# The RWKV-7 recurrence of a hybrid encoder layer, rewritten in slots: four phases of units, sums on opposite array halves, whole 64x64 inverses

## What is computed

```python
def wkv7_scan(r, w, k, v, kk, a, reverse):
    def step(state, inp):
        r_t, w_t, k_t, v_t, kk_t, a_t = inp
        sa = jnp.einsum('bhvk,bhk->bhv', state, -kk_t)
        state = (state * w_t[:, :, None, :]
                 + sa[..., None] * (kk_t * a_t)[:, :, None, :]
                 + v_t[..., None] * k_t[:, :, None, :])
        return state, jnp.einsum('bhvk,bhk->bhv', state, r_t)
    ...
    _, y = lax.scan(step, state0, xs, reverse=reverse)
```

## Time and profile before

| | us |
|---|---|
| median of 3 runs (1201.49 to 1203.64) | 1202.27 |
| span of the profiled execution, first to last instruction | 1183.8 |
| its TensorE busy | 1136.2 (96%) |
| the `scan` stage in it, first to last matmul | 516.0 to 623.7 |
| busy in 516.00 to 623.80: TensorE, VectorE, ScalarE, GpSimd | 105.57, 78.20, 50.56, 33.78 |

### The profile page before, as it was taken

One profiled execution on the slowest core, in us unless ns is written; L12 is line 12 of the kernel. 1 busy time (PEld: TensorE's weight loads), 2 busy tenths in 40 slices (PEclk: granted clock), 3 DMA queues, 4 the chain that ended last, 5 costly groups with the idle time before them and its releaser, 6 DMA issues. The chain is left out here.

```text
span 1183.8 us, 23882 instructions
## 1 busy us (share of the span) xinstructions
PE 1136.2 (96%) x9610; PEld 630.5 (53%) x9610; DVE 559.3 (47%) x1361; ACT 309.9 (26%) x793; POOL 254.2 (21%) x330
## 2 busy tenths in 40 slices
PE   6999999999999889889999999999899999999997
PEld 5534444444444457679895455664444444455553
DVE  4349526799969465556783444563111111111111
ACT  5054123522230377744451212300000000000000
POOL 0200410030000133633300001242345511112211
PEclk9989999999999999999999999999999999999999
DMA  9320343151220373436634841359999999777333
GB/s 342 97 51 26 104 140 87 36 178 36 89 54 36 90 188 103 132 102 179 162 90 178 286 180 72 134 210 414 406 349 336 381 337 343 293 285 293 136 135 114
DMA packets 109704, 213.19 MB, mean 180 GB/s; under 512 B 36516, under 2 KB 72836, under 8 KB 105752
## 3 DMA queue, kind: packets, MB, share of 16 engines
q1 hardware_dynamic: 81480, 127.19, 30.8%
q0 software_dynamic: 20192, 52.99, 13.7%
q10 hardware_dynamic: 7920, 31.46, 7.7%
HBM read 182.43 MB, written 35.58 MB: 184 GB/s over the span
## 5 line engine op out<-in xcount | busy, mean ns | idle before, releaser
L526 PE MATMUL pj_ps<-hT,pj_w 128*128 128x512 f32 x576 | 253.8, 597 | 0.0
L526 PEld LDWEIGHTS pj_ps<-hT,pj_w 128*128 128x128 f32 x576 | 108.2, 191 | 136.0 <-issue 135.4
L1464 PE MATMUL ps_out<-w_out,mixT 128*128 128x512 f32 x256 | 112.3, 594 | 2.1 <-PEq L2693 1.8
L2309 PE MATMUL ex_py<-wd,ex_hT 128*128 128x512 f32 x256 | 113.1, 592 | 0.0
L2458 ACT ACTIVATE ex_sg<-ex_pg 128x512 f32<-128x512 f32 x16 | 9.6, 597 | 272.8 <-PE ex_pg L2363 272.8
L738 DVE RECIPROCAL mixT<-mixT 128x1024 f32<-128x1024 f32 (+1 forms) x11 | 68.9, 6262 | 24.2 <-ACT mixT L658 19.2
L1464 PEld LDWEIGHTS ps_out<-w_out,mixT 128*128 128x128 f32 x256 | 47.8, 190 | 59.5 <-issue 59.4
L2377 PE MATMUL ex_pu<-proj 128*128 128x512 f32 x176 | 78.2, 592 | 0.0
L2363 PE MATMUL ex_pg<-proj 128*128 128x512 f32 x176 | 77.6, 594 | 0.0
L2572 DVE TENSOR_TENSOR ex_hid<-ex_pu,ex_sg 128x512 f32<-128x512 f32 x16 | 11.1, 691 | 136.1 <-PE ex_pu L2377 136.1
L2309 PEld LDWEIGHTS ex_py<-wd,ex_hT 128*128 128x128 f32 x256 | 47.1, 190 | 52.8 <-issue 52.8
(11 more groups left out here) (374 smaller groups left out, 1963.1 us busy)
## 6 DMA issues: line engine op xcount, KB each, us to landing
wd<-in_moe_w_down ACTq DMA_DIRECT2D x15, 2048.0 KB, 10.2
proj<-in_moe_w_gate SPq DMA_DIRECT2D x11, 2048.0 KB, 10.6
proj<-in_moe_w_up SPq DMA_DIRECT2D x11, 2048.0 KB, 12.2
mixT<-in_moe_w_gate SPq DMA_DIRECT2D x5, 2048.0 KB, 10.8
mixT<-in_moe_w_up SPq DMA_DIRECT2D x5, 2048.0 KB, 9.9
pj_w<-in_w_in SPq DMA_DIRECT2D x18, 512.0 KB, 4.0
proj<-in_x SPq DMA_DIRECT2D x16, 512.0 KB, 10.5
products<-pj_unit POOLq DMA_DIRECT2D x4, 2048.0 KB, 9.3
```

The source lines that it names most:

```text
L526: mm = pe.matmul(ps[:, t % 2, half, :], w_tile(t)[:, n, :], s.hT[:, n, half * 512:(half + 1) * 512], start=(n == 0), stop=(n == KD - 1))
L1464: mm = pe.matmul(s.ps_out[:, t % 2, half * 512:(half + 1) * 512], s.mixT[:, k, t * P:(t + 1) * P], s.w_out[:, k, half * 512:(half + 1) * 5 ...
L2309: mm = pe.matmul(py[:, half, :], hT[:, j, :], wd[e % 2][:, j, half * 512:(half + 1) * 512], start=(j == 0), stop=(j == KF - 1))
```

## The change

It replaces `scan` and what feeds it.

- **Slots.** TensorE now goes through 64 slots, one for each unit-step, the units in turn. Slot g makes the products of unit-step g+4, the right side of g, the solution of g-1 and state and output of g-2. So a unit-step's own phases lie in slots g-4, g, g+1 and g+2, with other units' work between them.
- **Halves.** Right side, solution and output are across pairs (`across_ps`). Products and the state's sums are straight (`straight_ps`). The output leaves with its heads exchanged, which `rwkv_out` undoes in its own matmuls.
- **Whole inverses.** In slots g-3 and g-2 two more pairs of 32 columns (`half_corner`, `corner`) fill in the off-diagonal 32x32 block of the inverse. The solution is then one pair in place of three, and `LOW`'s addition on VectorE is gone.
- **Products.** The second copy of the factors with exchanged halves is gone (GpSimd's 64 loads of it too). Products are two straight pairs of 128 columns; two transposes of 64 columns are made with the constant `fold`. VectorE masks 256 columns, ScalarE copies the other 128.
- **Loads.** Factors come with two loads a step (128x2x256 in place of 128x2x192), four steps deep. The inverses of four steps come with 12 loads, in two layouts that the projection stage stores (8 stores in place of 4).
- **Moved work.** The scaling of the state before the update and two of the normalising steps go from ScalarE and VectorE to GpSimd. GpSimd also clears the inverses' tiles at the stage's start.

The core of the diff:

```diff
-             l_mask_f=384, l_mask_b=384, below=32, iota=64, limits=14, token=8, keys=VCOLS, odd=1)
+             l_mask_f=256, l_mask_b=256, below=32, iota=64, limits=14, token=8, keys=VCOLS, odd=1)
...
-                for d, src in enumerate((ti[p], am[p])):
-                    sp.dma_start(s.t_dram[p, d * 64:(d + 1) * 64], src[d * 64:(d + 1) * 64, :, :].rearrange("p i j -> p (i j)")).then_inc(t_stored, 16)
+                for d, (turned, plain) in enumerate(((ti[p], am[p]), (am[p], ti[p]))):
+                    sp.dma_start(s.t_dram[d, :, :, p].rearrange("h g u b m -> (h g) (u b) m"), turned[d * 64:(d + 1) * 64, :, :].rearrange("p i j -> p (i j)")).then_inc(t_stored, 16)
+                    sp.dma_start(s.plain_dram[d, :, :, p].rearrange("h g u m -> (h g) u m"), plain[d * 64 + d:(d + 1) * 64:2, :, :].rearrange("p i j -> p (i j)")).then_inc(t_stored, 16)
...
-                dve.tensor_copy(am[p][64:128, :, :], ti[p][64:128, :, :].rearrange("p i j -> p j i")).then_inc(finished, 1)
+                dve.tensor_copy(am[p], ti[p].rearrange("p i j -> p j i")).then_inc(finished, 1)
...
+GROUP = 4
+INVERSE_LOADS, PLAIN_LOADS = 8, 4
+GROUP_IN = 16 * (INVERSE_LOADS + PLAIN_LOADS)
+def load_factors(sp, s, i):
     row = 4 * CHUNK
     for d in range(2):
+        src = bass.AP(s.p_dram.tensor, (2 * d * NCH + step_chunk(i, d)) * P * row, [[row, P], [NCH * P * row, 2], [1, row]])
+        sp.dma_start(s.units[i % 4][:, 2 * d:2 * d + 2, :, :].rearrange("p n f t -> p n (f t)"), src).then_inc(s.unit_in[i % 4], 16)
+def group_place(i, d):
+    return i % GROUP if d == 0 else GROUP - 1 - i % GROUP
+def first_chunk(g, d):
+    return GROUP * g if d == 0 else NCH - GROUP * (g + 1)
+def load_inverses(sp, s, g, n):
+    d, (h, half) = n // 4, HALVES[n % 4]
+    src = s.t_dram[d, h, first_chunk(g, d) // GROUP].rearrange("p u b (i j) -> i (p u) b j", j=SIDE)[:, :, half, :]
+    q = 2 * (1 - h) + half
+    dst = s.inverses[g][q * SIDE:(q + 1) * SIDE, 2 * d:2 * d + 2, :, half * SIDE:(half + 1) * SIDE]
+    sp.dma_start(dst.rearrange("p n u j -> p (n u) j"), src).then_inc(s.inverse_in[g], 16)
+def load_plain(sp, s, g, n):
+    d, h = n // 2, n % 2
+    src = s.plain_dram[d, h, first_chunk(g, d) // GROUP].rearrange("p u (i j) -> i (p u) j", j=SIDE)
+    q = 2 * h + d
+    sp.dma_start(s.plain[g][q * SIDE:(q + 1) * SIDE, 2 * d:2 * d + 2, :, :].rearrange("p n u j -> p (n u) j"), src).then_inc(s.inverse_in[g], 16)
...
+            def straight(out, left, right, start, stop):
                 for p0, p1 in HEADS:
+                    mm = pe.matmul(out[p0:p1], left[p0:p1], right[p0:p1], start=start, stop=stop)
+                return mm
+            def across(out, left, right, start, stop):
                 for h, (p0, p1) in enumerate(HEADS):
                     q0, q1 = HEADS[1 - h]
+                    mm = pe.matmul(out[q0:q1], left[p0:p1], right[p0:p1], start=start, stop=stop)
+                return mm
+            def first_part(x):
+                n, i, d, p, ch = place(x)
+                if n == 0:
+                    pe.wait_ge(s.unit_in[i % 4], 32 * (i // 4 + 1))
+                if x >= NU:
+                    pe.wait_ge(copied, x - NU + 1)
+                    pe.wait_ge(s_out, x - NU + 1)
+                    pe.wait_ge(t_out, x - NU + 1)
+                f = s.units[i % 4]
+                straight(straight_ps[:, n, LT * HD:(M5 + 1) * HD], f[:, n, F_K, :], f[:, n, F_A:F_K, :].rearrange("p f t -> p (f t)"), True, True)
+            def right_side(g):
+                n, i, d, p, ch = place(g)
+                pe.wait_ge(masked, g + 1)
+                pe.wait_ge(s_out, g + 1)
+                if g >= NU:
+                    pe.wait_ge(y_out, g - NU + 1)
+                across(across_ps[:, n, W:W + HD], lm[:, i % 2, n, LT, :], vt[:, p, ch, :], True, False)
+                across(across_ps[:, n, W:W + HD], s.units[i % 4][:, n, F_A, :], st[:, n, :], False, True).then_inc(w_sum, 1)
+            def transposes(x):
+                n, i, d, p, ch = place(x)
+                f = s.units[i % 4]
+                straight(straight_ps[:, n, KT * HD:(KT + 1) * HD], f[:, n, F_K, :], s.fold, True, True)
+                straight(straight_ps[:, n, BT * HD:(BT + 1) * HD], f[:, n, F_B, :], s.fold, True, True)
+            def solution(m):
+                n, i, d, p, ch = place(m)
+                pe.wait_ge(w_out, m + 1)
+                pe.wait_ge(t_out, m + 1)
+                mm = across(u_sums(n), s.inverses[i // GROUP][:, n, group_place(i, d), :], wt[:, n, :], True, True)
+                if m + NU >= TOTAL:
                     mm.then_inc(u_sum, 1)
+            def second_part(x):
+                n, i, d, p, ch = place(x)
+                f = s.units[i % 4]
+                straight(straight_ps[:, n, CT * HD:(M1 + 1) * HD], f[:, n, F_B, :], f[:, n, F_A:F_K, :].rearrange("p f t -> p (f t)"), True, True).then_inc(prods, 1)
+            def old_output(l):
+                n, i, d, p, ch = place(l)
+                pe.wait_ge(u_out, l + NU + 1)
+                across(across_ps[:, n, Y:Y + HD], s.units[i % 4][:, n, F_R, :], st[:, n, :], True, False)
+            def half_corner(x):
+                n, i, d, p, ch = place(x)
+                if x % (NU * GROUP) == 0:
+                    pe.wait_ge(s.inverse_in[i // GROUP], GROUP_IN)
+                pe.wait_ge(masked, x + 1)
+                across(z_sums(n), lm[:, i % 2, n, CT, :], s.plain[i // GROUP][:, n, group_place(i, d), :], True, True).then_inc(u_sum, 1)
+            def corner(x):
+                n, i, d, p, ch = place(x)
+                pe.wait_ge(copied, x + 1)
+                pe.wait_ge(u_out, x + 1)
+                mm = straight(straight_ps[:, n, OFF:OFF + SIDE], z_of(n), s.inverses[i // GROUP][:, n, group_place(i, d), later(d)], True, True)
+                if x < NU:
                     mm.then_inc(y_sum, 1)
+            def outputs(l):
+                n, i, d, p, ch = place(l)
+                v, u = vt[:, p, ch, :], u_of(n)
+                straight(straight_ps[:, n, STATE:STATE + HD], lm[:, i % 2, n, KT, :], v, True, False)
+                across(across_ps[:, n, Y:Y + HD], lm[:, i % 2, n, M5, :], v, False, False)
+                straight(straight_ps[:, n, STATE:STATE + HD], lm[:, i % 2, n, BT, :], u, False, True)
+                across(across_ps[:, n, Y:Y + HD], lm[:, i % 2, n, M1, :], u, False, True).then_inc(y_sum, 1)
+            pe.wait_ge(started, 2)
+            for g in range(-AHEAD, TOTAL + 2):
+                if g + AHEAD < TOTAL:
+                    first_part(g + AHEAD)
+                if 0 <= g < TOTAL:
+                    right_side(g)
+                if g + AHEAD < TOTAL:
+                    transposes(g + AHEAD)
+                if 0 <= g - 1 < TOTAL:
+                    solution(g - 1)
+                if g + AHEAD < TOTAL:
+                    second_part(g + AHEAD)
+                if 0 <= g - 2:
+                    old_output(g - 2)
+                if 0 <= g + 3 < TOTAL:
+                    half_corner(g + 3)
+                if 0 <= g + 2 < TOTAL:
+                    corner(g + 2)
+                if 0 <= g - 2:
+                    outputs(g - 2)
...
+            def mask(x):
+                n, i, d, p, ch = place(x)
+                dve.wait_ge(prods, x + 1)
+                if x >= 2 * NU:
+                    dve.wait_ge(y_sum, x - 2 * NU + NU + 1)
+                dve.tensor_tensor(lm[:, i % 2, n, CT:BT, :].rearrange("p f c -> p (f c)"), straight_ps[:, n, MADE:MADE + BT * HD], s.l_mask[d], ALU.mult).then_inc(masked, 1)
...
+            for g in range(1 - AHEAD, TOTAL + 3):
+                if g + 3 < TOTAL:
+                    mask(g + 3)
+                if 0 <= g - 3:
+                    update(g - 3)
+                i = g // NU
+                if i < NCH:
+                    if g % NU == 2 and FINAL <= i - 1:
+                        sums(i - 1)
+                    if g % NU == 2 and FINAL <= i - 3:
+                        invert(i - 3)
+                    if g % NU == 0 and FINAL <= i - 2:
+                        spread(i - 2)
...
+            def place_corner(x):
+                n, i, d, p, ch = place(x)
+                act.wait_ge(y_sum, x + 1)
+                act.wait_ge(s_out, x + 1)
+                act.activation(s.inverses[i // GROUP][:, n, group_place(i, d), later(d)], straight_ps[:, n, OFF:OFF + SIDE], ACT.Copy).then_inc(t_out, 1)
+            def negate(g):
+                m = g - 1
+                n = m % NU
+                ahead = m + NU < TOTAL
+                act.wait_ge(u_sum, m + NU + 1)
+                if m >= 0 and ahead:
+                    dst, src = uz[:, n, 0:HD + SIDE] if n < 2 else uz[:, n, SIDE:2 * HD], across_ps[:, n, U:U + HD + SIDE]
+                elif ahead:
+                    dst, src = z_of(n)[:, 0:SIDE] if n < 2 else z_of(n)[:, SIDE:HD], z_sums(n)
+                else:
+                    dst, src = u_of(n), u_sums(n)
```

(25 more changed lines are left out.)

315 lines of the change are left out of this document (118 added, 197 removed).

## The result

The changed kernel takes 1206.4 us (20 runs, 1201.88 to 1210.57), the kernel before 1201.45 (20 runs, 1193.91 to 1205.42). The ratio is 1.0048, with an interval of 1.0032 to 1.0063: slower by half a per cent, where 1170 us and 0.89 for faster had been forecast.

What follows compares the result with a forecast made beforehand. It took one half of TensorE's array to bound the recurrence. Start 0.6, lead-in 3.0, 64 slots of 1.07, statistics 2.0 and end 1.1 make 75.2 us against 107.7, so 1170 us; range 1161 to 1176, or 1162 to 1186 with waits.

Steps and rivals of the forecast that it cites:

- TensorE's new sum: Recurrence slot: straight half 0.97 us, across half 0.77, overlapping, so the slot is the longer; 1.07 us taken with waits.
- the chains of waits: Dependences between a slot's engines: the tightest needs 0.65 us of a 0.97 us slot, so every chain fits.
- What bounds the kernel now: Recurrence before: one array half bounds it; a unit-step's pairs sum to 1.49 us, measured 1.68, the rest waits.
- That rival: Recurrence: straight and across halves take turns, slot 1.74 us, stage 119 us, time 1214 us; chance 0.08.
- Matmuls of 32 columns: Short pairs in a slot: no trace showed one; priced between 0.066 and 0.117 us each, slot 0.97 to 1.02.
- Other engines: VectorE and ScalarE in a slot: some 0.75 us with overlap and 0.95 before overlap, neither exceeding 0.97.
- Statistics, start and loads: Recurrence: statistics 2 us, GpSimd's copies at the start 0.6 us, factor loads hidden with 0.7 us to spare.
- late-factors rival: Recurrence loads: factors land late, six slots last 8.1 us, stage 94 us, time 1189 us; chance 0.05.
- The gain is given back: Behind the recurrence: a later stage does not start earlier, so the time stays the same; chance 0.03.
- The 18.5 us around it stay: Outside the profiled span: 18.5 us between span and median are unchanged, so median 1202.27 becomes 1169.8 us.
- The sum: Whole recurrence: terms add to 75.2 us against 107.7, so 32.5 us saved.

Runs made afterwards that it cites:

- lean_padded: merged_lean with one extra 32-column across matmul a slot, 256 TensorE instructions more in all; ratio to the kernel before 0.9911, stage 102.8 us.
- after_again: The changed kernel, unchanged, run and profiled a second time; 1204.99 us, ratio to the kernel before 1.0049, stage 118.0 us.
- before_again: The kernel before, unchanged, profiled a second time; 1199.72 us, stage 113.6 us.
- before_third: The kernel before, unchanged, profiled a third time; 1204.51 us, stage 113.8 us.
- merged_lean: merged without those TensorE waits that an earlier wait already covers, same matmuls; 1180.47 us, ratio to the kernel before 0.9809, stage 95.7 us.
- fewer_across: The changed kernel without the output's product of masked factors with values, one across pair a slot; only the stage is read, 111.5 us.
- merged: The changed kernel with the two transposes folded into the products, two pairs a slot fewer; 1193.32 us, ratio to the kernel before 0.9933.
- after_lean: The changed kernel with only TensorE's redundant waits dropped; ratio to the kernel before 0.9983, stage 110.9 us.
- wide: The changed kernel with 192 in place of 128 columns in each slot's first products, same instruction number; 1203.16 us, ratio to the kernel before 1.0041.
- quiet: The changed kernel with the twelve `w_out` loads moved from the stage to behind it; 1215.2 us, stage 117.0 us.
- burst: The changed kernel with 512 matmuls of 32 columns added ahead of the first slot; stage 151.5 us.

## Why the prediction was wrong

**The failed step is TensorE's new sum**, as the prediction put it: "the slot is the longer of the two: 0.97", and 64 times 1.07 for the stage. It priced a slot by the array's two halves and the chains of waits, and had no term for the supply of instructions. The halves do overlap and the chains do fit: a slot between pauses is 1.03 us, and the stage less its pauses 72.2 and 77.2 us, where 75.2 had been worked out. What was left out, a term put at nothing, is 44 to 46 us of pauses, 29 blocks of 256 instructions at some 1.55 us each.

Why there was no such term is instructive. The change cuts the array's time for a unit-step, from 1.49 to 0.97 us by the prediction's sum, and *raises* its instructions: 28 matmuls (four records each, a load and a matmul twice) in place of 24, and 271 separate semaphore instructions in the stage in place of 97. Before, 6241 records in 107.8 us are 58 a microsecond. The forecast's stage would have needed 7439 in 75.2, 99 a microsecond. One block each 4.1 us is 62. The rates could have been read from the trace of before: the earlier trace rows have the count of matmuls and loads beside the time, and its page the instruction queue. What they would not have told is the limit: the rate of 58 ran with two stops at a block's edge, half a microsecond each. The earlier trace rows did mislead here: they show four-quarter use over 64 matmul records, with their loads 128 instructions, which is half a block.

**Point by point.**
- *What bounds the kernel now.* "One half of the array, and the other half is used by one pair in twelve" fits the stage before, where 105 to 107 us lie between the pauses, but no run adds columns alone to that kernel. The stage of before already showed 4 to 8 pauses. One reading was off: the earlier trace rows leave out the record in which the products' first across matmul starts,

```profile
565.78 0.38 PE L1290 MATMUL sc_ps<-proj 64*64 64x192 f32 x2
```

so that the four matmuls lie within 0.40 us, not 0.32. The straight pair alone has the 0.32 on which the new sum rests, and that stands.
- *The Trainium skill's rule that a weight load overlaps running matmuls only where their row groups differ* ("TensorE: Matmul & The Clock Gate", Part 3) did not lead to the outcome that the prediction took from it: straight and across matmuls of the same rows start 0.02 us apart in the timeline above, and the halves did not take turns. That rival had 1214 us and is the only one that said slower, for a wrong reason: its slot of 1.74 us would show in every slot, and the trace shows 1.03 and then a stop.
- *Matmuls of 32 columns* "between 0.066 and 0.117": no run measures the array's price of one alone. With free array time what one costs is its four instructions (lean_padded, 0.11 us a slot).
- *Other engines.* VectorE's mask took 0.424 us (0.417 worked out). ScalarE's copies took 0.223, 0.193, 0.282 and 0.251 (0.95 in all, as forecast). Neither engine fills the stage: 57.46 and 49.76 of 121.5.
- *Statistics, start and loads* were near what had been charged or hidden. Of after_again's late slots without a stop some last 1.36 to 1.46 us, 0.3 to 0.4 above the others. The first matmul waits 1.57 us for GpSimd's copies, where it waited 1.14 for the sequencer before. Factors land 3.3 us after issue, 5.3 at most, and no wait of TensorE for them shows. The late-factors rival fell.
- *The gain is given back* fell too: behind the stage there are 562.1 and 558.8 us (563.2 and 562.4 in before_again and before_third), so what the stage gains comes out at the end. merged_lean's 18 us against before_again in the stage are 22 in the time, each time against its own kernel before.
- *"The 18.5 us around it stay"* was wrong, as before_again showed: 2 us. Most of it cancels, since the forecast subtracts a saving from a median. What does not is the stage: from a typical one of 113.7 us to 75.2 the same working would have saved 38.5 us, not 32.5.
- *The sum, corrected*: from before_again to the changed kernels the part between pauses gives 28 to 33 us, and the pauses take 36 to 38. The stage is 4 to 8 us longer, the time 5.8 (1.0048 of 1201).

**What is shown and what is not.** Shown: pauses at nearly every 256th TensorE instruction, each ended by a fetch; a stage that gets shorter with fewer instructions (fewer_across, merged, merged_lean, after_lean) and longer with more (lean_padded), and does not move with the array's time (wide) or with a quarter less of the other DMA traffic (quiet). Not shown: a fixed price for a block. For each 256 instructions fewer the stage lost 3.3 to 5.0 us in fewer_across, 1.6 to 2.4 in merged, 7 to 11 in after_lean and 14 to 16 in merged_lean. Nor is it shown what fixes the 4.1 us. A fetch itself takes 1.1 us, TensorE goes on 2.2 us or more after its start (median 2.5), and the next one starts 1.3 to 2.1 us after that (median 1.6, changed kernel). With 2.5 us to execute a block this leaves the 1.5 of a stop. In the lean kernels blocks come every 3.8 to 4.0 us. Whether the wait before a fetch is for room in the instruction memory or the sequencer's own pace, and why leaving out semaphore instructions shortens it, no run separates.

## What to carry to other kernels

Beside an engine's busy time, count its instructions in the stretch and divide by the time that you forecast. A change that shortens matmuls, or runs several at once, meets a supply of some 61 to 65 TensorE instructions a microsecond in these stages (57 to 59 in merged, 74 in burst's slow part); from there on a column was free here and an instruction was not: merge matmuls, let one moving operand do two jobs, and drop waits that an earlier wait covers. Idle time put down to "issue" that comes at even distances in records, on an engine whose operands are ready, was this limit here.

Take a second profile of the kernel before, with its own time, before a difference of 1% is forecast from it: this one was 16 us short of the median.

## What the runs showed of the hardware

- TensorE's instructions come in blocks of 256 (16.4 KB each on the instruction queue), one each 3.8 to 4.4 us in the dense stages; the stop at a block's end lasts 1.2 to 3.0 us in the changed kernel. In burst, at the lower clock, a block came every 3.5 us.
- From the start of a fetch to TensorE's next instruction behind a stop it is some 2.5 us, and from there to the start of the next fetch 1.2 to 1.7 (medians, by kernel).
- TensorE issues 256 instructions in about 2.5 us between two stops: 72.2 us for 7439 are 9.7 ns each.
- A float32 matmul of 64 by 64 is four instructions, with 32 columns as with 256. With one more a slot the stage grew by 7.1 us, or 0.11 us a slot, for 32 columns.
- A matmul that waits for more than one semaphore costs extra instructions: leaving 240 redundant waits out was worth 0.7% to 1.2% of the whole kernel.
- The granted clock was 0.52 in 25 us of little but 32-column matmuls, though TensorE counted as busy for 22.95 of them. It had fallen after 6 us with 3.47 busy.
